# Where the sums of weight blocks are kept in the second feed-forward part of a decoder step

## The reference

```python
def _swiglu(x, w_gate, w_up, w_down):
    return (jax.nn.silu(x @ w_gate) * (x @ w_up)) @ w_down

def _layer(h, pos, h0_re, h0_im, ckv_past, krope_past, p):
    h = h + 0.5 * _swiglu(_rms(h, p['g_ffn1']), p['w_ffn1_gate'], p['w_ffn1_up'], p['w_ffn1_down'])
    mix, ... = _mixer(_rms(h, p['g_mix']), ...)     # S5 scan and latent attention
    h = h + mix
    h = h + 0.5 * _swiglu(_rms(h, p['g_ffn2']), p['w_ffn2_gate'], p['w_ffn2_up'], p['w_ffn2_down'])
```

## Time and profile before

| What | Value |
| --- | --- |
| three runs | 1411.57, 1423.03, 1425.56 us (median 1423.03) |
| profiled execution | 1403.47 us, its span 1401.6 us |
| busy, whole span | PE 1303.8 us (93%), PEld 1201.2, DVE 799.0 (57%), ACT 509.9 (36%), POOL 391.7 (28%) |
| granted TensorE clock | 0.975 of 2.4 GHz over the span |
| second feed-forward part | first tile from 944 us, products from 971 to 1365 us |
| mean DVE time, 953 to 992 us | L1539, L1542, L1548 1.29 us each; L1613 0.72; L1533 0.95 (four, one of them stretched) |
| mean ACT time, 953 to 992 us | L886 0.62 us, L895 1.10, L928 silu 0.66, L944 copy 0.38 |
| classical tiles on TensorE | tile 1 ends 952.9, tile 2 959.8, tile 3 runs from 963.90; a tile takes about 6.0 us |
| first split of x on VectorE (L1539) | starts 961.83; the third x scaling before it ends at 959.15 |

### The profile page before, as it was taken

How to read it: one execution, slowest core, us unless ns; L and a number is a source line. 1 busy time by engine, 2 the same in 40 slices (tenths; PEclk the granted TensorE clock), 3 DMA queues, 4 the chain that set the end, 5 groups by cost and what they waited for, 6 DMA issues and landing times.

```text
span 1401.6 us, 28495 instructions
## 1 busy us (share of the span) xinstructions
PE 1303.8 (93%) x11292; PEld 1201.2 (86%) x11292; DVE 799.0 (57%) x1373; ACT 509.9 (36%) x949; POOL 391.7 (28%) x417
## 2 busy tenths in 40 slices
PE   7999999999999999999999999996888888898887
PEld 7999999999999989677676669996888888798887
DVE  6334335324347995444444655548778678668664
ACT  5232221221234222333233333444553444345344
POOL 0229245129111112522222200231234124223302
PEclk9999999999999999999999999998899999899988
DMA  6223222223224223689999985333556665664631
GB/s 233 83 83 105 82 69 76 91 71 95 76 76 174 69 69 97 222 303 332 337 333 324 332 309 202 110 100 75 143 119 138 153 140 121 149 158 114 140 89 64
DMA packets 101992, 212.22 MB, mean 151 GB/s; under 512 B 12785, under 2 KB 26514, under 8 KB 101554
## 3 DMA queue, kind: packets, MB, share of 16 engines
q1 hardware_dynamic: 87586, 184.51, 40.6%
q0 software_dynamic: 11264, 19.41, 7.8%
q10 hardware_dynamic: 3024, 6.69, 1.2%
HBM read 200.87 MB, written 9.69 MB: 150 GB/s over the span
## 4 chain that ended last, share of the span: by engine, by line
PE 63%; DVE 12%; DMA 10%; issue 7%; POOL 4%; ACT 3%; SPq 1%; ACTq 0%; DVEq 0%; POOLq 0%
PE d L2157 36%; PE e L2502 5%; PE d L2264 4%; PE e L2264 4%; DMA kv<-kv_src 4%; DMA wr<-w_gu 4%; DVE ws_lo L1522 3%; PE e L2534 2%; DVE w_lo L1413 2%; DMA wr<-w_d2b 1%; SPq L545 1%; PE e L2553 1%; PE d L2566 1%; ACT ws_hi L886 1%; PE d L2177 1%
## 5 line engine op out<-in xcount | busy, mean ns | idle before, releaser
L1413 DVE TENSOR_TENSOR w_lo<-raw,w_hi 128x1024 fp32r<-128x1024 f32 (+2 forms) x127 | 151.9, 1196 | 201.1 <-ACT w_hi L770 200.3
L770 ACT CAST w_hi<-raw 128x1024 fp32r<-128x1024 f32 (+2 forms) x127 | 123.6, 973 | 296.8 <-PE d L2157 279.4
L1522 DVE TENSOR_TENSOR ws_lo<-wr,ws_hi 128x512 fp32r<-128x512 f32 (+1 forms) x224 | 168.8, 757 | 91.9 <-ACT ws_hi L886 86.4
L2157 PE MATMUL d<-x_hi,w_hi 128*128 128x272 f32 x976 | 205.8, 292 | 13.7 <-DVE w_lo L1761 6.8
L2157 PE MATMUL d<-x_hi,w_lo 128*128 128x272 f32 x976 | 203.7, 290 | 0.0
L2157 PE MATMUL d<-x_lo,w_hi 128*128 128x272 f32 x976 | 203.1, 290 | 0.0
L886 ACT CAST ws_hi<-wr 128x512 fp32r<-128x512 f32 (+1 forms) x224 | 123.4, 580 | 155.1 <-PE d L2264 43.2
L2157 PEld LDWEIGHTS d<-x_hi,w_hi 128*128 128x128 f32 x976 | 155.4, 190 | 16.4 <-DVE w_lo L1761 6.8
L2157 PEld LDWEIGHTS d<-x_lo,w_hi 128*128 128x128 f32 x976 | 155.2, 191 | 0.0
L2157 PEld LDWEIGHTS d<-x_hi,w_lo 128*128 128x128 f32 x976 | 154.2, 191 | 0.0
L1388 POOL DMA_INDIRECT kr<-kr_src,gidx x64 | 61.0, 954 | 173.2 <-PE e L2537 162.4
(11 more groups left out here) (435 smaller groups left out, 3190.2 us busy)
## 6 DMA issues: line engine op xcount, KB each, us to landing
kv<-kv_src SPq DMA_DIRECT2D x256, 256.0 KB, 4.5
wr<-w_gu SPq DMA_DIRECT2D x100, 256.0 KB, 3.2
raw<-w_gu SPq DMA_DIRECT2D x47, 512.0 KB, 3.6
raw<-w_post SPq DMA_DIRECT2D x34, 512.0 KB, 3.8
wr<-w_gu POOLq DMA_DIRECT2D x40, 256.0 KB, 4.5
wr<-w_d2b SPq DMA_DIRECT2D x40, 192.0 KB, 2.8
raw<-w_d1b SPq DMA_DIRECT2D x16, 384.0 KB, 3.3
raw<-w_in SPq DMA_DIRECT2D x10, 512.0 KB, 3.7
```

The source lines that it names most:

```text
L770: nc.scalar.copy(w_hi[:, s % 2, 0:n, :], raw[:, raw_pos(s), 0:n, :]).then_inc(S.hi_done, 1)
L1413: nc.vector.tensor_tensor(w_lo[:, s % 2, 0:n, :], raw[:, raw_pos(s), 0:n, :], w_hi[:, s % 2, 0:n, :].bitcast(FP), ALU.subtract).then_inc(S ...
L1522: nc.vector.tensor_tensor(ws_lo[k % NWS][:, 0:steps(n), :], wide(n, FROM[typ]), ws_hi[k % NWS][:, 0:steps(n), :].bitcast(FP), ALU.subtract ...
L2157: ins = mm(out[:, b, :], w[:, pos, c0 + k, :], x[:, k, b * HALF:(b + 1) * HALF], start=first, stop=stop)
```

## The change

Five things change. (1) The first sum, X + A22, is written into A11's buffer once P1 is split, and the second, A12 + A11, into A12's buffer; P6 is split from A11, P3 from A12. (2) VectorE makes both sums in all units, behind the splits of P7 and of P2; GpSimd makes none, and issues the accumulation of X before that of Y. (3) There are eleven weight buffers: A22 has three, the others two, and the due times of the loads are new. (4) `sl` and `upb` have three buffers each; the third lies where the high and low parts of x were, over the last two low parts of the tail's weights. (5) In the hand-over several steps of ScalarE and VectorE stand at other places: tile 1 is emptied earlier, P1, P7 and P6 of unit 0 are copied between the first splits, and the last two splits of x come behind the first products.

```diff
     lh_lo = inside("lh_lo", [NLAST, TOK], FR, tail, NLAST * T4, TAIL)
-    sl = inside("sl", [2, TOK], FP, rt, 0, RT)
-    upb = inside("upb", [2, TOK], FP, rt, 2 * T4, RT)
+    sl = [inside("sl%d" % i, [TOK], FP, start, offset, size) for i, (start, offset, size) in enumerate(((rt, 0, RT), (rt, T4, RT), (rx, 4 * H7, RX)))]
+    upb = [inside("upb%d" % i, [TOK], FP, start, offset, size) for i, (start, offset, size) in enumerate(((rt, 2 * T4, RT), (rt, 3 * T4, RT), (rx, 4 * H7 + T4, RX)))]
+    NSL = len(sl)
     hv = inside("hv", [8, HALF], FP, rt, 4 * T4, RT)
     x_t1 = inside("x_t1", [KC // 2, HALF], FP, rt, 4 * T4 + 3 * T4 // 2, RT)
 
 
     KW = 4
-    NWR, NWS = 10, 8
+    NWR, NWS = 11, 8
     early = TAIL - 3 * 2048 - 3 * 4096
     assert early >= 2 * NLAST * T4 and early >= 2 * H7 and early >= 8 * T4
...
-    FROM = {"P1": "A11", "P2": "A12", "P7": "X", "P6": "X", "P3": "X", "P4": "A22", "P5": "Y"}
+
+    HELD = {"A11": (0, 5), "X": (1, 6), "A12": (2, 7), "A22": (3, 9, 10), "Y": (4, 8)}
+    FROM = {"P1": "A11", "P2": "A12", "P7": "X", "P6": "A11", "P3": "A12", "P4": "A22", "P5": "Y"}
     READ = {"A11": (0, 0), "A12": (0, 1), "A22": (1, 1), "X": (0, 0), "Y": (1, 0)}
     ADDED = {"X": (1, 0), "Y": (1, 1)}
+    LAST_READ = {"A11": "P6", "A12": "P3", "X": "P7", "A22": "P4", "Y": "P5"}
+    LAST_HELD = (("X", NU), ("A11", NU), ("A22", NU), ("Y", NU), ("X", NU + 1), ("A12", NU), ("A11", NU + 1), ("A22", NU + 1))
 
     def weight_block(n, row, half):
 
...
+        return HELD[x][n % len(HELD[x])]
 
     def wide(n, x):
...
 
-        typ = {"A11": "P1", "A12": "P2", "X": "P3", "A22": "P4", "Y": "P5"}[x] if "X" in HELD else {"A11": "P3", "A12": "P2", "A22": "P4", "A21": "P5"}[x]
-        return [after("w_lod", AT[typ, n] + 1)] + [(S.s4_sum, n + 1)] * (x == "A12")
+        sums = {"A11": [(S.s4_sum, n + 1)], "X": [(S.s2_sum, n + 1)]}
+        return [after("w_lod", AT[LAST_READ[x], n] + 1)] + sums.get(x, [])
+
+    def before(n, x):
+        return n - len(HELD[x])
 
...
@@ -729,28 +730,29 @@
             post(s)
         def weight_load(n, x):
 
-            if n >= 2:
-                for w in read_last(n - 2, x):
+            if before(n, x) >= 0:
+                for w in read_last(before(n, x), x):
                     sp.wait_ge(*w)
             elif held(n, x) >= 3:
                 sp.wait_ge(S.lo_done, S_FFN2 + (held(n, x) - 3) // 2 + 1)
             sp.dma_start(wide(n, x), weight_block(n, *READ[x]).rearrange("p (c n) -> p c n", n=P)).then_inc(sem[WR_IN[held(n, x)][0]], 16)
 
...
         for n, x in first_loads:
             weight_load(n, x)
         for i in range(2 * HEAD):
             slot(S_FFN2 + i, a["w_gu2"][2 * tile_of(i // 2) + i % 2], 8)
-        when = {"A11": 0, "A12": 4.5, "Y": 6.5, "X": 9.5, "A22": 12.5}
+        when = {"A11": 4.5, "A12": 9.5, "Y": 6.5, "X": 1.7, "A22": 5.5}
         for n in range(2):
-            for x in ("A11", "X", "A12", "Y", "A22"):
+            for x in ("A11", "X", "A22", "A12", "Y"):
                 if (n, x) not in first_loads:
                     weight_load(n, x)
...
+            def product_out(k):
+                typ, n = ORDER[k]
+                act.wait_ge(*after("pr", k + 1))
+                if not dense(n):
+                    j = pair_of(n)
+                    if typ == "P1":
+                        if j >= NSL:
+                            act.wait_ge(*after("mul", j - NSL + 1))
+                        nc.scalar.copy(sl[j % NSL][:, 0:HALF], bank(n, 0)).then_inc(S.p1_out, 1)
+                    if typ == "P7":
+                        nc.scalar.copy(upb[j % NSL][:, HALF:TOK], bank(n, 2)).then_inc(S.p7_out, 1)
+                    if typ == "P6":
+                        nc.scalar.copy(upb[j % NSL][:, 0:HALF], bank(n, 0)).then_inc(S.p6_out, 1)
+                    if typ == "P3":
+                        nc.scalar.activation(sl[j % NSL][:, HALF:TOK], bank(n, 0), ACT.Silu).then_inc(S.c12, 1)
+
             part_hi(0)
             split_hi(s + 2, t + 1, n=8)
             root(N_FFN2, 0, D_MODEL)
             split_hi(s + 3, t + 2, n=8)
             part_hi(1)
             act.wait_ge(S.evac, t + 1)
-            nc.scalar.activation(sl[:, 0, :], sl[:, 0, :], ACT.Silu).then_inc(S.slu, 1)
-            for i in range(3):
-                x7_split_hi(i)
+            nc.scalar.activation(sl[0][:, :], sl[0][:, :], ACT.Silu).then_inc(S.slu, 1)
+            x7_split_hi(1)
             part_hi(2)
+            x7_split_hi(2)
+            part_hi(3)
+            x7_split_hi(3)
             act.wait_ge(S.evac, t + 3)
-            nc.scalar.activation(sl[:, 1, :], sl[:, 1, :], ACT.Silu).then_inc(S.slu, 1)
-            x7_split_hi(3)
-            part_hi(3)
+            nc.scalar.activation(sl[1][:, :], sl[1][:, :], ACT.Silu).then_inc(S.slu, 1)
             x7_split_hi(4)
             part_hi(4)
-            x7_split_hi(5)
+            product_out(0)
             part_hi(5)
+            product_out(1)
             part_hi(6)
             part_hi(7)
-            x7_split_hi(6)
+            product_out(2)
             for k, (typ, n) in enumerate(ORDER):
-                act.wait_ge(*after("pr", k + 1))
-                if not dense(n):
-                    j = pair_of(n)
-                    if typ == "P1":
-                        act.wait_ge(*after("mul", j - 1))
-                        nc.scalar.copy(sl[:, j % 2, 0:HALF], bank(n, 0)).then_inc(S.p1_out, 1)
-                    if typ == "P7":
-                        nc.scalar.copy(upb[:, j % 2, HALF:TOK], bank(n, 2)).then_inc(S.p7_out, 1)
-                    if typ == "P6":
-                        nc.scalar.copy(upb[:, j % 2, 0:HALF], bank(n, 0)).then_inc(S.p6_out, 1)
-                    if typ == "P3":
-                        nc.scalar.activation(sl[:, j % 2, HALF:TOK], bank(n, 0), ACT.Silu).then_inc(S.c12, 1)
+                if k > 2:
+                    product_out(k)
                 part_hi(k + NWS)
+                if k == 0:
+                    x7_split_hi(5)
+                if k == 2:
+                    x7_split_hi(6)
...
@@ -1248,12 +1262,6 @@
             pool.dma_start(wide(n, x), weight_block(n, *ADDED[x]).rearrange("p (c n) -> p c n", n=P), accum_op=ALU.add
                            ).then_inc(sem["acc_%s%d" % (x.lower(), n % 2)], 16)
 
-        def add_in_place(n, x, typ, done):
-
-            pool.wait_ge(*after("w_lod", AT[typ, n] + 1))
-            pool.wait_ge(*landed(n, x))
-            nc.gpsimd.tensor_tensor(wide(n, "X"), wide(n, "X"), wide(n, x), ALU.add).then_inc(done, 1)
-
         def ffn2():
             def hidden(j):
...
@@ -1277,12 +1285,9 @@
                 hidden(j)
             for n in range(-1, NU):
                 if 2 <= n + 2 < NU:
+                    add_block(n + 2, "X")
+                if 2 <= n + 2 < NU:
                     add_block(n + 2, "Y")
-                if n + 1 < NU and dense(n + 1):
-                    add_in_place(n + 1, "A22", "P7", S.s2_sum)
-                    add_in_place(n + 1, "A12", "P6", S.s4_sum)
-                if 2 <= n + 2 < NU:
-                    add_block(n + 2, "X")
                 if n >= 1 and not dense(n - 1):
                     hidden(pair_of(n - 1))
             last_squares()
...
             dve.wait_ge(*after("w_hid", k + 1))
+            if k >= NP + 6:
+                dve.wait_ge(*after("mul", sum(BLOCKS) - 1))
...
             typ, n = ORDER[k]
             nc.vector.tensor_tensor(ws_lo[k % NWS][:, 0:steps(n), :], wide(n, FROM[typ]), ws_hi[k % NWS][:, 0:steps(n), :].bitcast(FP),
                                     ALU.subtract).then_inc(S.w_lod, 1)
-            if typ == "P7" and not dense(n):
-                add_in_place(n, "A22", k, S.s2_sum)
-            if typ == "P6" and not dense(n):
-                add_in_place(n, "A12", k, S.s4_sum)
-
-        def add_in_place(n, x, k, done):
-
-            dve.wait_ge(*after("w_lod", k + 1))
-            dve.wait_ge(*landed(n, x))
-            nc.vector.tensor_tensor(wide(n, "X"), wide(n, "X"), wide(n, x), ALU.add).then_inc(done, 1)
+            if typ == "P7":
+                dve.wait_ge(*landed(n, "A22"))
+                dve.wait_ge(*after("w_lod", AT["P1", n] + 1))
+                nc.vector.tensor_tensor(wide(n, "A11"), wide(n, "X"), wide(n, "A22"), ALU.add).then_inc(S.s2_sum, 1)
+            if typ == "P2":
+                dve.wait_ge(S.s2_sum, n + 1)
+                dve.wait_ge(*after("w_lod", k + 1))
+                nc.vector.tensor_tensor(wide(n, "A12"), wide(n, "A12"), wide(n, "A11"), ALU.add).then_inc(S.s4_sum, 1)
...
             split_lo(s + 3, n=8)
             x_scaled(0, 0)
             x_scaled(1, 1)
+            evacuate(1)
             x_scaled(2, 3)
             x_sum(x_t1[:, :, :], xn[:, 1, :, :], xn[:, 3, :, :], ALU.subtract, 1)
             x_sum(xn[:, 1, :, :], xn[:, 0, :, :], xn[:, 1, :, :], ALU.subtract, 2)
             x7_split_lo(0)
-            evacuate(1)
```

(18 more changed lines are left out.)

## The result

The changed kernel took **1353.57 us** (median of four runs, 1352.11 to 1354.33); the kernel before took 1417.79 us beside it (four runs). The ratio is 0.9543, 95% interval 0.9484 to 0.9603: faster by 4.6%. The forecast was 1370 us, from 1350 to 1404. The medians are 64 us apart; the prediction had summed 53. Three of the four runs of before are the three that stand ahead of the prediction.

What follows compares the result with a forecast made beforehand. TensorE bounds the kernel, with 68 us lost in the loop largely behind late X. Loop 46 us (68 less residual 22) plus hand-over 7 made 53, off the 1423.0 us median: 1370 us, range 1350 to 1404.

Steps and rivals of the forecast that it cites:

- The bound and the mechanism: Second feed-forward loop: TensorE bounds; late X holds ScalarE's and VectorE's in-order queues, within 68 us excess over 282 us work.
- under 10 was named: Sign of being right: ScalarE's rounding waits for weight transfers (`wr`) fall from 63.9 us to under 10.
- The residual: Loop excess left after the change: 13.5 us in gate units plus 8.4 in dense, together 22; saved 46 us.
- VectorE's price: 24 sums moved to VectorE cost 13 to 17 us, up to 16 freed; net -3 to +17, taken as 0.
- The margin of VectorE: Dense units: VectorE's work 6.9 us beside TensorE's 7.9, so TensorE stays the bound with little to spare.
- the rival (0.17): Loop: units run at VectorE's pace, the residual doubles to 45 us; 1393 us, chance 0.17.
- Buffers: Third chunk buffers gain nothing beyond the 68 us; A22's three buffers give ten slots, at least 10.1 us, for its load.
- the slower rival: Every unit: VectorE blocks at the sum waiting for A22, 20 us added; 1436 us, chance 0.06.
- The hand-over: Before the loop: P6 at 975.3 instead of 986.20, P7 of unit 2 about 998.6; gain 7 us, bounds 3 and 11.
- The baseline: The 53 us were subtracted from the three-run median 1423.0 us; the profiled execution, 1403.5, lay 19.6 us below it.
- the new sums could block `hv`: First two dense units of a block: each GpSimd `hv` would lose up to 0.69 us, hidden by slots.
- the tail: End of the kernel: `hv`, lh_hi, lh_lo still hold TensorE 2.56 us; last two low parts wait nothing or 1 us.

Runs made afterwards that it cites:

- Run 1: Changed kernel with only the due time of X's load put back from 1.7 to 9.5: 1413.53 us, ratio 1.0053 to the kernel before.
- run 3: Changed kernel with the dense units' two sums on GpSimd, behind its issues of X and Y: 1367.24 us, ratio 0.9716 to the kernel before.
- run 4: The kernel of run 3 with Y's accumulation issued behind the two sums, X's still ahead: 1345.31 us, ratio 0.9594 to the kernel before.
- run 8: Changed kernel with the hand-over's ScalarE and VectorE steps in the order of before: 1343.97 us, ratio 0.9539 to the kernel before.
- run 2: Kernel before, sums still in place in X, but VectorE also makes those of the dense units: 1398.87 us, ratio 0.9940 to the kernel before.
- run 5: Changed kernel with the first sum of every unit made four times on VectorE: 1380.82 us, ratio 0.9845 to the kernel before.
- run 7: Changed kernel with two chunk buffers (`sl`, `upb`) instead of three: 1355.06 us, ratio 0.9563 to the kernel before.
- run 6: Changed kernel with two A22 buffers instead of three and A22's due time at 12.5: 1362.38 us, ratio 0.9630 to the kernel before.
- run 9: Changed kernel with another hand-over order: ScalarE's first product copies earlier, VectorE's last x sum and x7_lo(6) later: 1342.83 us, ratio 0.9578 to the kernel before.
- run 10: The kernel of run 9 with the fourth x scaling and last x sum on GpSimd, second `h_lo` two products later: 1347.09 us, ratio 0.9516 to before.

## Why the prediction was right, and where it was off

**The bound and the mechanism: right.** X was late, P5 stopped behind ScalarE's and VectorE's queues, and an earlier X removed all of it. The waits went from 63.9 us to none (under 10 was named), the clock in the loop to 1.00 (0.98 was named), the matmuls of the loop to 291 us (305 was named). Run 1 shows that the due time is indispensable. It does not show it to be all: run 3 keeps it and loses 22 us. That VectorE or GpSimd makes the sums is worth 3 us (run 4), the hand-over 2 to 4 (run 8).

**The residual: mis-sized.** I put 22 us (nine waits of 1.5 us, and 0.7 a dense unit); measured are 291 - 282 = 9. Of the nine chunk pairs only three make P7 wait, 1.49 us lost each (1.3 of it idle), one in each block (units 4, 14 and 24), and the dense units have no loss but one wait for `h_lo` at the first unit of each group, 1.02 to 1.05 us lost (0.9 idle). I had taken the longer of two observed waits for all nine, though the earlier trace rows showed only two in all; these six make 7.6 us. The rest of the 9 is in matmuls that start a little later than 0.1253 us behind the one before; the clock is granted in full throughout the loop, so none of it is half clock. The saving was 59 us, not 46.

**VectorE's price: the sums right, the return undercounted.** 24 sums at 0.55 us are 13.3 us, as costed (13); 15.7 us came back from splits that are no longer stretched (up to 16), and 7.0 from the sums of `hv`, which the prediction did not count among the stretched: net -9, below the range of -3 to +17. In before five of these sums took 1.25 to 2.08 us, each beside a sum of GpSimd (L1255), and the others 0.44; in run 2, where GpSimd makes no sums, all of them are at 0.44. What the prediction did not price is the place in GpSimd's queue. With X and Y issued first, sums left on GpSimd would have cost 22 us (run 3), 19 of them for standing behind a waiting issue (run 4). The order "X, then Y, then the multiplication" is harmless here, with no urgent work behind it.

**The margin of VectorE: overrated.** Busy 247 of 291 us looks like 44 us to spare; run 5 shows some 20. In the dense units I had 6.9 us of VectorE's work beside 7.9 of TensorE's; measured are 7.9 of 8.24 us (busy 96% from P7 to P7), since pairs of split and `h` at 0.82 us leave out the sums of `hv`, the drains of the gate unit before, the wider splits and sums of the gate unit behind, and the stretching that stayed (splits of 128x384 take 0.617 us in the mean for 0.55). So TensorE holds the dense units by 0.3 us a unit. That the forecast had room for the rival (0.17) was well; that it did not come true was close.

**Buffers: right.** Three chunk buffers 0 (run 7). Three buffers for A22, with an earlier due time, were the cover for its load; without them 11 us are lost (run 6), by the mechanism that I gave the slower rival.

**The hand-over: 2 to 4 us instead of 7.** 3 was the lower bound. P6 of unit 0 came where it was forecast: 32.1 us after the first rounding is 976.2 on before's scale, against 975.3. The step that failed is the next one, "By the same adding it empties P4's bank at 998.3, and P7 of unit 2 starts about 998.6": it skips P3 of unit 0, which waits 6.27 us for P5's drain (L1606). That drain stands behind the second sum, x7_lo(5), a split, the x sum and x7_lo(6), which themselves wait 1.23 us for ScalarE. Runs 5 and 9 say why neither of two new orders helps: VectorE's 51 us of work set the length, as far as added work can show it. I added durations along one path and never added up the engine.

**The baseline.** I subtracted from the median (1423.0) and not from the profiled execution (1403.5). Before's median beside the change was 1417.8, which bears that out, though three of its four runs are the same ones; on two other chips it was 1406.0 and 1402.4, so the base hangs on the chip. From the profiled execution the same 53 us would have given 1350.5, 3 us off instead of 16, but by luck: that execution was 11.5 us shorter ahead of the part that the change touches, which hides most of the 10 us by which the saving was put too low. The forecast of 1370 missed by 16 us: 5 from that median, 13 from the loop, 1.5 from the tail, less 3 to 5 for the hand-over.

**VectorE beside GpSimd.** The prediction held against the change that the new sums could block `hv`; no wait for `hv` shows in the loop, and GpSimd's `hv` takes 1583 ns in the mean of 18 before (L1271) and 1585 after (L1279), so no run shows a loss by it. Run 10 shows the other direction, 5.42 us for 1.29 and 2.99 for 0.68. The Trainium skill ("SBUF — State Buffer", Who interferes with whom) says that a VectorE instruction with two SBUF inputs contends with a GpSimd instruction that reads SBUF, that the shared ports are an exclusive lock, and that the order of issue decides who blocks. The blocking agrees with that; of the order the trace shows that the 5.42 us instruction started 0.11 us ahead of GpSimd's first and still ended behind both.

## What to carry to other kernels

A buffer that comes free earlier was worth nothing here until the load's place in the issuing queue moves too, and urgent work should not stand in an in-order queue behind an issue that waits for a landing. Where an engine is busy for 51 of 60 us, as VectorE here, add up its work first and leave the order for later. And add it up by stage: 247 of 291 us hid units in which VectorE was busy 96%. Work moved from VectorE to GpSimd can come back as longer instructions of VectorE.

## What the runs showed of the hardware

Beside GpSimd's two-input instructions two of VectorE's in run 10 look stopped rather than slowed: 0.68 us became 2.99, 1.29 became 5.42, each ending within 1.3 us of GpSimd's end and longer by about what GpSimd was busy (2.4 and 4.2 us). Five sums of 0.44 us in before took 1.25 to 2.08, each beside a sum of GpSimd. The accumulation of gate units landed later in the changed kernel, 5.3 us in the median for 4.6, and the plain load of 256 KB 4.3 for 3.3; the DMA engines were 70% busy in the loop instead of 58. But load alone does not explain it: in run 1 the accumulation took 6.3 us at 54% busy, and the dense units' `w_d2b` accumulation of 192 KB stayed at 4.0 us for 4.1, though the share in the dense windows rose from 0.6 to 0.8. What sets it stays open.
